# A layer with convolution and sparse attention on one core: the gating product changes engine, the convolution's start is tied to the weight casts, the channel norm is pipelined, and maxima are placed later

## The chip, the cores and the metric

The kernel runs on one core of a Trainium2 chip. The metric is the device time of one execution in microseconds (us). TensorE is called PE below, VectorE DVE, ScalarE ACT, GpSimd POOL, and SyncE, which only issues transfers here, SP. A name such as `gt` in a row is a tile (`gt` those of the gate stage, `cv` the convolution's, `nm` the norm's, `at` the attention's), `scratch_...` is a buffer in DRAM, and a name such as L1042 is a line of the kernel before.

## The reference

One layer over 2048 prompt positions and 64 sample positions, 2112 columns in all, with 1024 channels. What touches the change:

```python
z = h @ w_in
a_conv, g_conv, q, k, v, g_attn, qi, ki, wi, gm = split_in(z)
# conv_branch: u, then a causal depthwise convolution of 31 taps, LayerNorm over channels, silu
u = a[..., :D_CONV] * jax.nn.sigmoid(a[..., D_CONV:])
y = conv(u) + conv_b
y = jax.nn.silu(layernorm(y, ln_g, ln_b))
y_c = (y * jax.nn.silu(g_conv)) @ w_conv_out
# attend_block: for each query the 256 best keys by an index score, then softmax over these
score = jnp.where(admissible[None], score, -jnp.inf)
_, idx = lax.top_k(score, top_k)
```

## The kernel before, in words

The program is a row of stages, each with one instruction stream per engine and a barrier at its end: setup, rows, scores, **gate**, **norm**, **attention**, branch, output. The change lies in the three in bold.

**Gate stage.** PE multiplies the activations `ha` with 56 blocks of 128 weight columns, once for each half of the 2112 columns: blocks 0 to 55 for the first half, 56 to 111 for the second. Block n belongs to pair m = n // 2. One block is 72 matmuls of 352 columns (three split products, L1042), and two PSUM buffers alternate, so PE starts block n only when ACT has evicted block n-2. In the first half POOL splits each block's weights into a high and a low part (`cast`, L600 and L602), and ACT stores both parts to `scratch_ws`; in the second half ACT fetches them back (`fetch`), and issues the fetch for block n+2 right behind the eviction of block n. Each half begins with the eight pairs of kind `u` (pairs 0 to 7 and 28 to 35): one block is the sigmoid part, the other the plain part; ACT evicts them to `stage[0]` and `stage[1]`, and POOL forms their product in `ustage` (`gated`, L1011) and stores it to `scratch_u` (L1014). ACT evicts the next pair only when that product is done. The pair behind the last `u` pair waits in ACT for all `u` products.

Meanwhile ACT and DVE search thresholds for the 256 best keys of each query: 32 rounds of bisection, in each of which ACT counts for the query tiles of the tuple `SCALAR` (L813) and DVE for those of `VECTOR` (L842), after which DVE decides (L850 and following). ACT's rounds stand between its evictions, seven in eight blocks. Then DVE writes the masks (up to L905), and then convolves: eight steps k, four for each half of the columns, each of two channel groups with 31 taps, so 62 instructions (L1168 two, L1172 sixty). The loads of `u` and the stores of `y` are issued by SP; those of step 4 wait for all 16 products to be stored.

**Norm stage.** Five chunks (four of 512 columns, one of 64) of 8 x 128 channels. For each: PE sums (L1232), DVE subtracts the mean (L1269), ACT squares (L1252), PE sums the squares (L1242), DVE adds epsilon (L1275), ACT takes the square root (L1254), DVE the reciprocal (L1278) and one Newton step (L1280 to L1283) and scales (L1284), ACT applies silu (L1257, eight instructions), DVE multiplies with the gate (L1287), POOL stores (L1220). The `y` tiles have two buffers, but each engine's stream goes through one chunk after the other.

**Attention stage.** 68 units (four key-value groups times 17 query tiles) with 308 block pairs, one pair a step. PE's stream is written step by step from a plan: scores of the step's pair (L1602 to L1614), values of the pair two steps earlier (L1633 to L1635), and between them matmuls for the row maxima of a later unit (L1656), which go through a ring of two PSUM banks and are reduced by DVE (L1776). The maxima of unit u need `qhi[u % 3]`, which POOL casts (L1556, L1558) as soon as the last scores of unit u-3 are done. `opens` is the first step in which maxima of unit u may stand: `last[u - 3] + 1`; from there they are dealt two or three to a step, or up to four where they are due. POOL also prepares `near` tiles between the maxima (L1571, L1572), and, inside units 8 to 12 of each group but the last, the keys and values of the next group (L1520 to L1551).

Of the kernel before, what the change touches and what calls it, by code (L numbers as in the profile page):

```python
# [785 lines left out]
class Search:  # L786


    SCALAR = (15, 12, 6, 14, 11, NT)
    VECTOR = (13, 9, 7, 2, 10, 8, 5, 4, 3)  # L790
# [117 lines left out]
def gate_stage(nc, mem, w, scr, scores, kept):  # L908
# [3 lines left out]
    with ExitStack() as ctx:  # L912
# [3 lines left out]
                           + [([P, KC, P], F32R)] * 4 + [([P, W], F32)] * 3  # L916
# [3 lines left out]
        raw, whi, wlo, stage, ustage = parts[1:3], parts[3:5], parts[5:7], parts[7:9], parts[9]  # L920
        junk, equal, junk2, rank = parts[10:14]
        cells = {"count": parts[14], "goal": parts[15], "short": parts[16], "value": parts[17],
                 "candidate": parts[18], "taken": parts[19], "flip": parts[20], "bit": parts[21], "limbs": parts[22]}
        assert mem.at["gt22"] + 20 * ntk <= mem.high([([P, KC, W], F32R)] * 2)
# [80 lines left out]
        def _(pool):  # L1005
            def gated(m):
# [5 lines left out]
                half, _, i = pairs[m]  # L1012
                pool.wait_ge(s_u, u_done[m + 1])
                pool.dma_start(scr["u"][i * P:(i + 1) * P, half * W:(half + 1) * W], ustage[:]).then_inc(s_ustore, 16)  # L1014

            for m, (half, kind, i) in enumerate(pairs):
                for b in range(2):
                    if half == 0:
                        if m:
                            pool.wait_ge(s_wst[b], 32 * m)  # L1020
                        pr.cast(pool, b, m)
                if kind == "u" and i:
                    gated(m - 1)
                if kind == "u" and i == KC - 1:
                    gated(m)

# [35 lines left out]
        def _(act):  # L1062
            def evict(m, b):
# [78 lines left out]
        def _(dve):  # L1142
# [5 lines left out]

            for k in range(8):
# [14 lines left out]
                for k_ in range(CONV_W):  # L1164
                    for e, (c, mine, to) in enumerate(both):
# [7 lines left out]
                        ins.then_inc(s_tap, 1)  # L1173
                dve.wait_ge(s_tap, base + TAPS)
# [3 lines left out]
def norm_stage(nc, mem, out, scr):  # L1178
# [3 lines left out]
    with ExitStack() as ctx:  # L1182
        sem = lambda n: ctx.enter_context(nc.semaphore("norm_" + n))
        CW = 512
        parts = mem.layout("nm", [([P, total + MASKPAD], BF16)] + [([P, KC, CW], F32)] * 5 + [([P, CW], F32)] * 4
                           + [([P, KC, 2, STATE], F32)] + [([STATE, 2, D], F32)])
        y, sq, gc = parts[1:3], parts[3], parts[4:6]
        var, inv, tmp, _ = parts[6:10]
        tails, states = parts[10:12]

        chunks = [(c, c, CW) for c in range(0, SEQ, CW)] + [(SEQ + STATE, SEQ, DEC)]
        s_y, s_gc = [sem("y0"), sem("y1")], [sem("gc0"), sem("gc1")]
        s_store = [sem("store0"), sem("store1")]
        s_mean, s_var, s_sq, s_dve, s_sqrt, s_silu, s_out = (sem(n) for n in ("mean", "var", "sq", "dve", "sqrt", "silu", "out"))
        s_tail, s_tt, s_st = sem("tail"), sem("tt"), sem("st")
        block = ctx.enter_context(nc.Block())
        PER = 8

        @block.sync
        def _(sp):  # L1200
            tail_of = scr["u"].rearrange("(c p) t -> p c t", p=P)
            for k, end in enumerate((SEQ, T)):
                sp.dma_start(tails[:, :, k, :], tail_of[:, :, end - STATE:end]).then_inc(s_tail, 16)
            for n, (col, tok, width) in enumerate(chunks):
                b = n % 2
                if n >= 2:
# [966 lines left out]
```

## Time and profile before

| | us |
|---|---|
| median of 3 runs | 4201.15 |
| lowest and highest | 4200.99 and 4205.64 |
| profiled execution, its own time | 4206.21 |
| its span in the trace | 4204.5 |
| PE busy | 3544.8 (84%) |
| DVE busy | 2776.7 (66%) |
| POOL busy | 1389.7 (33%) |
| ACT busy | 1361.2 (32%) |

The profiled execution took 1.7 us more than its span and 5.1 us more than the median. The busy share of PE is an average over stages; in the gate stage PE is the engine that the others feed, in the norm stage it idles for most of the time.

### The profile page before, as it was taken

To read this page: it belongs to the slowest core of one execution; us is meant where nothing else is said; L and a number is where in the kernel's file an instruction comes from. 1 tells how busy PE (TensorE), PEld (TensorE's weight loads), DVE (VectorE), ACT (ScalarE), POOL (GpSimd) and SP (SyncE) were. 2 spreads that over 40 slices of the span, in tenths; PEclk is the share of its full clock that TensorE was granted. 3 is DMA by queue.
4 is the path that set the end of the run, shared out by engine and by line. 5 is a ranking of instruction groups with operands and counts; after the bars stand their busy time and mean duration, and the time that the engine had idled before them with its cause. 6 is when DMAs were issued, how large, how long until landed. Compare 5 with 4: busy or idle time off the path is not lost. (4 is left out here: it accounts for less than half of the span.)

```text
span 4204.5 us, 49713 instructions
## 1 busy us (share of the span) xinstructions
PE 3544.8 (84%) x18895; PEld 2949.0 (70%) x18895; DVE 2776.7 (66%) x4232; ACT 1361.2 (32%) x1587; POOL 1389.7 (33%) x1050
## 2 busy tenths in 40 slices
PE   5967769899994858999942789989989997899789
PEld 1966559899994858999921455555555554899777
DVE  1412898878999992997034777777877775554244
ACT  2201667667200000010023355545545554000011
POOL 1333324533457271000000464454363342344200
PEclk9988999999997989999976799999999998999999
DMA  7573106545653514444343221201201112465533
GB/s 254 170 268 92 35 18 183 173 158 168 198 184 115 192 50 166 158 155 160 126 147 120 64 51 29 65 26 31 63 26 29 33 31 94 127 227 182 179 109 118
DMA packets 381304, 502.12 MB, mean 119 GB/s; under 512 B 47304, under 2 KB 287064, under 8 KB 380507
## 3 DMA queue, kind: packets, MB, share of 16 engines
q1 hardware_dynamic: 253211, 212.58, 17.1%
q10 hardware_dynamic: 114672, 237.76, 16.9%
q0 software_dynamic: 13264, 49.85, 3.4%
q8 instruction: 78, 1.28, 0.1%
q14 instruction: 79, 0.65, 0.1%
HBM read 306.67 MB, written 199.73 MB: 120 GB/s over the span
## 5 line engine op out<-in xcount | busy, mean ns | idle before, releaser
L1042 PE MATMUL psum<-ha,gt 128*128 128x352 f32 x8064 | 1326.2, 326 | 164.1 <-POOL gt L602 88.4
L1042 PEld LDWEIGHTS psum<-ha,gt 128*128 128x128 f32 x8064 | 1320.2, 190 | 169.9 <-POOL gt L602 78.6
L1172 DVE SCALAR_TENSOR_TENSOR cv<-cv,vecs,cv 128x1056 f32<-128x1056 f32 (+1 forms) x480 | 606.4, 1342 | 0.0
L1827 DVE TENSOR_TENSOR at_plo<-at,at 128x1024 fp32r<-128x1024 f32 (+2 forms) x308 | 390.7, 1269 | 142.5 <-ACT at L1727 141.1
L1726 ACT ACTIVATE at<-psum 128x1024 f32<-128x1024 f32 (+2 forms) x308 | 293.2, 952 | 524.1 <-PE psum L1614 523.9
L1656 PE MATMUL psum<-at,at 128*128 128x512 f32 (+5 forms) x688 | 349.3, 513 | 131.8 <-POOL at L1558 57.1
L613 PE MATMUL psum<-br,br 128*128 128x352 f32 x2304 | 376.1, 325 | 42.4 <-DVE br L1941 41.1
L613 PEld LDWEIGHTS psum<-br,br 128*128 128x128 f32 x2304 | 375.5, 189 | 42.8 <-DVE br L1941 41.2
L842 DVE TENSOR_SCALAR_CACHE_REDUCE gt<-sc,gt 128x1792 bf16<-128x1792 f32 (+9 forms) x294 | 350.1, 1258 | 1.2
L813 ACT ACTIVATE gt<-sc,gt 128x2048 bf16<-128x2048 f32 (+2 forms) x192 | 298.4, 1555 | 67.8 <-issue 59.8
L1079 ACT ACTIVATE gt<-psum 128x1056 f32<-128x1056 f32 x80 | 83.9, 1049 | 716.2 <-PE psum L1042 695.8
L600 POOL TENSOR_TENSOR gt<-gt,ones 128x1024 fp32r<-128x1024 f32 x56 | 183.5, 3277 | 382.3 <-DMA scratch_ws<-gt 180.4
L1727 ACT ACTIVATE at<-psum 128x1024 fp32r<-128x1024 f32 (+2 forms) x308 | 290.8, 944 | 0.0
L1776 DVE CUSTOM_DVE_ANT_0 at<-psum,cv 128x512 bf16<-128x512 f32 (+4 forms) x416 | 237.6, 580 | 75.2 <-PE psum L1656 68.9
L1656 PEld LDWEIGHTS psum<-at,at 128*128 128x128 f32 x688 | 139.2, 203 | 197.1 <-POOL at L1558 71.6
L1602 PE MATMUL psum<-at,at 128*128 128x512 f32 (+1 forms) x580 | 245.5, 423 | 0.0
L1633 PE MATMUL psum<-at,at 128*65 128x512 f32 (+1 forms) x580 | 231.5, 399 | 1.7 <-ACT at L1739 0.8
L1605 PE MATMUL psum<-at,at 66*128 66x512 f32 (+1 forms) x580 | 229.3, 395 | 0.0
L1635 PE MATMUL psum<-at_plo,at 128*65 128x512 f32 (+1 forms) x580 | 227.9, 393 | 0.0
L1634 PE MATMUL psum<-at,at 128*65 128x512 f32 (+1 forms) x580 | 227.5, 392 | 0.0
L1614 PE MATMUL psum<-at,cv 128*128 128x512 bf16 (+1 forms) x580 | 226.4, 390 | 0.0
L1220 POOL DMA_DIRECT2D scratch_c<-nm x5 | 4.5, 897 | 655.0 <-DVE nm L1287 655.0
(229 smaller groups left out, 5236.2 us busy)
## 6 DMA issues: line engine op xcount, KB each, us to landing
scratch_ws<-gt ACTq DMA_DIRECT2D x112, 512.0 KB, 6.1
gt<-scratch_ws ACTq DMA_DIRECT2D x112, 512.0 KB, 5.1
gt<-in_w_in_dram ACTq DMA_DIRECT2D x56, 512.0 KB, 5.3
scratch_gm<-gt ACTq DMA_DIRECT2D x32, 528.0 KB, 3.1
br<-scratch_gm ACTq DMA_DIRECT2D x32, 528.0 KB, 3.6
scratch_m<-br POOLq DMA_DIRECT2D x32, 528.0 KB, 4.4
at<-scratch_q SPq DMA_DIRECT2D x128, 128.0 KB, 2.8
su<-in_ada_w_dram SPq DMA_DIRECT2D x6, 2048.0 KB, 22.3
```

The lines of the kernel that those rows point to most:

```text
L613: last = self.nc.tensor.matmul(self.psum[b][:, j, 0:W // 3], w[b][:, c, :], a[:, c, j * (W // 3):(j + 1) * (W // 3)], start=(c == 0 and k ...
L813: nc.scalar.activation(junks[(done + k) % 2][:, 0:keys_of(t)[1]], part_of(scores, t), ACT.Sign, bias=cells["candidate"][:, j:j + 1].bitcas ...
L842: nc.vector.tensor_scalar(junks[k % 2][:, 0:keys_of(t)[1]], part_of(scores, t), threshold[:, j:j + 1].bitcast(F32), None, compare, ALU.add ...
L1042: ins = nc.tensor.matmul(psum[b][:, j, 0:W // 3], wt[b][:, c, :], a[:, c, j * (W // 3):(j + 1) * (W // 3)], start=(c == 0 and k == 0), sto ...
L1172: ins = nc.vector.scalar_tensor_tensor(to[:, 0:width], mine[:, k_:k_ + width], tap, to[:, 0:width], ALU.mult, ALU.add)
L1602: nc.tensor.matmul(dst, kst[g % 2][:, keys], qhi[u % 3][:, 0:n], start=True, stop=False)
L1633: nc.tensor.matmul(acc[0:VW, 0:n], vst[g % 2][:, v, 0, :], phi[j % 3][:, k, 0:n], start=(b == 0), stop=False)
L1656: nc.tensor.matmul(bank(("max", u, h, c))[:, 0:w], qhi[u % 3][:, at:at + P], kst[g % 2][:, key0:key0 + w], start=True, stop=True).then_inc ...
L1726: nc.scalar.activation(prob[j % 3][:, 0:len(mine), 0:n], src, ACT.Exp)
L1727: nc.scalar.activation(phi[j % 3][:, 0:len(mine), 0:n], src, ACT.Exp).then_inc(s_phi, 1)
L1776: nc.vector.tensor_tensor_reduce(out=junk[r % 2][:, 0:w], in0=bank(("max", u, h, c))[:, 0:w], in1=other, scale=1.0, scalar=LOWEST, op0=ALU ...
L1827: nc.vector.tensor_tensor(plo[j % 3][:, 0:len(mine), 0:n], prob[j % 3][:, 0:len(mine), 0:n], phi[j % 3][:, 0:len(mine), 0:n].bitcast(F32), ...
```

## The change

1. In the search, query tile 6 (896 keys) moves from ACT's tuple to DVE's, so ACT counts five tiles a round and DVE ten.
2. In the second half DVE forms the eight `u` products, each behind a fixed instruction of the convolution (behind number 96 + 18j, counted from 0 over all steps k); POOL only stores them. ACT evicts the `u` pairs of the second half alternately to `stage[0..1]` and `stage[2..3]`, so it may be one pair further ahead of the products. The pair behind the last `u` pair still waits for all of them.
3. DVE starts the convolution only when POOL has split the last weight block (number 55).
4. The norm has four `y` buffers, two PSUM banks for means and two for squares; the chunks are interleaved on each engine; the square root and reciprocal become exp(-0.5 ln(x)) on ACT, with the Newton step kept on DVE.
5. In the attention's plan the maxima of a unit open up to two steps later.

```diff
-    SCALAR = (15, 12, 6, 14, 11, NT)
-    VECTOR = (13, 9, 7, 2, 10, 8, 5, 4, 3)
+    SCALAR = (15, 12, 14, 11, NT)
+    VECTOR = (13, 9, 7, 2, 6, 10, 8, 5, 4, 3)
...
+            for m in range(half_pairs, half_pairs + KC):
+                store(m)
...
                 if kind == "u":
-                    if u_done[m] and b == 0:
+                    at = stage[b + 2 * (half * (m % 2))]
+                    if half == 0 and u_done[m] and b == 0:
                         act.wait_ge(s_u, u_done[m])
-                    if o_done[m]:
+                    if half and i >= 2 and b == 0:
+                        act.wait_ge(s_u, u_done[m] - 1)
+                    if half and o_done[m]:
                         act.wait_ge(s_store[b], 16 * o_done[m])
-                    nc.scalar.activation(thirds(stage[b], W // 3), psum[b][:, :, 0:W // 3], ACT.Copy if b else func).then_inc(pr.s_read, 1)
+                    nc.scalar.activation(thirds(at, W // 3), psum[b][:, :, 0:W // 3], ACT.Copy if b else func).then_inc(pr.s_read, 1)
                     return
                 if b == 0 and pairs[m - 1][1] == "u":
                     act.wait_ge(s_u, u_done[m])
...
+            def gated(m):
+
+                e = 2 * (m % 2)
+                dve.wait_ge(pr.s_read, 2 * (m + 1))
+                dve.wait_ge(s_ustore, 16 * u_done[m])
+                nc.vector.tensor_tensor(ustage[:], stage[e][:], stage[e + 1][:], ALU.mult).then_inc(s_u, 1)
+
+            dve.wait_ge(pr.s_split, BLOCKS)
+            gated_at = {96 + 18 * j: half_pairs + j for j in range(KC)}
...
+                        if step in gated_at:
+                            gated(gated_at[step])
+                        step += 1
...
+            load_y(0)
+            load_y(1)
+            load_gc(0)
...
+            load_y(2)
+            load_gc(1)
+            load_y(3)
...
+            for n in range(2, N):
+                load_gc(n)
+                if n + 2 >= YB and n + 2 < N:
+                    load_y(n + 2)
...
+            sums(0)
+            sums(1)
+            for n in range(N):
+                squares(n)
+                if n + 2 < N:
+                    sums(n + 2)
...
+                nc.scalar.activation(r, var[n % 2][:, 0:width], ACT.Ln, bias=eps[:]).then_inc(s_root, 1)
+                act.wait_ge(s_root, 2 * n + 1)
+                nc.scalar.activation(r, r, ACT.Exp, scale=-0.5).then_inc(s_root, 1)
...
+            square(0)
+            for n in range(N):
+                if n + 1 < N:
+                    square(n + 1)
+                root(n)
+                if n:
+                    swish(n - 1)
+            swish(N - 1)
...
+            centre(0)
+            centre(1)
+            for n in range(N):
+                scale(n)
...
+                if n + 2 < N:
+                    centre(n + 2)
+                if n:
+                    gated(n - 1)
+            gated(N - 1)
...
-            opens = self.last[u - 3] + 1 if u >= 3 else self.begin
+            opens = max(self.last[u - 3] + 1, min(self.last[u - 3] + 3, self.first[u] - 7)) if u >= 3 else self.begin
```

On DVE, in the convolution's step k = 1 of the changed kernel, the first of the eight products (L1162; `gt_4589` and `gt_4590` are `stage[0]` and `stage[1]`) stands here:

```order
L1190 SCALAR_TENSOR_TENSOR cv_4615<-cv_4611,vecs,cv_4615 128x1056
L1190 SCALAR_TENSOR_TENSOR cv_4614<-cv_4610,vecs,cv_4614 128x1056
L1162 TENSOR_TENSOR gt_4593<-gt_4589,gt_4590 128x1056
L1190 SCALAR_TENSOR_TENSOR cv_4615<-cv_4611,vecs,cv_4615 128x1056
L1190 SCALAR_TENSOR_TENSOR cv_4614<-cv_4610,vecs,cv_4614 128x1056
L1190 SCALAR_TENSOR_TENSOR cv_4615<-cv_4611,vecs,cv_4615 128x1056
```

It has 97 instructions of the convolution ahead of it; the eighth has 223. In the kernel before this product was POOL's, behind nothing.

On ACT in the norm stage, one chunk before (`nm_9344` is the squares' tile, `nm_9347` and `nm_9348` hold the variance and its root):

```order
L1252 ACTIVATE nm_9344<-nm_9342 128x4096
L1254 ACT_TABLE_LOAD
L1254 ACTIVATE nm_9348<-nm_9347 128x512
L1257 ACT_TABLE_LOAD
L1257 ACTIVATE nm_9342<-nm_9342,vecs 128x512 x8
```

and in the changed kernel, from the squares of the third chunk to the silu of the first:

```order
L1303 ACTIVATE nm_9347<-nm_9343 128x4096
L1311 ACT_TABLE_LOAD
L1311 ACTIVATE nm_9349<-psum,nm_9354 128x512
L1313 ACT_TABLE_LOAD
L1313 ACTIVATE nm_9349<-nm_9349 128x512
L1319 ACT_TABLE_LOAD
L1319 ACTIVATE nm_9341<-nm_9341,vecs 128x512 x8
```

The silu now works on a chunk two behind that of the squares, and there are three table loads for two.

On PE in the attention, at step 1 (scores of unit 1, then the shift row of unit 2 that both have; maxima of unit 3, whose `opens` was step 1), before:

```order
L1614 MATMUL psum<-at_9748,cv_4605 128x512
L1656 MATMUL psum<-at_9706,at_9721 128x512
L1602 MATMUL psum<-at_9722,at_9706 128x512
L1605 MATMUL psum<-at_9725,at_9708 128x512
L1614 MATMUL psum<-at_9748,cv_4605 128x512
L1656 MATMUL psum<-at_9706,at_9721 128x512
L1666 MATMUL psum<-at_9749,at_9746 66x128 x4
```

and the same scores in the changed kernel:

```order
L1705 MATMUL psum<-at_9753,cv_4607 128x512
L1693 MATMUL psum<-at_9727,at_9711 128x512
L1696 MATMUL psum<-at_9730,at_9713 128x512
L1705 MATMUL psum<-at_9753,cv_4607 128x512
L1757 MATMUL psum<-at_9754,at_9751 66x128 x4
```

The two maxima are gone from here and stand two steps later. Over the plan, 60 of the 68 units open two or three steps later; steps with four maxima go from 16 to 50, and steps with none from 27 to 60.

## Rows read from the trace of the kernel before

**Rows 1.** Busy time by stage; columns: PE, PEld, DVE, ACT, POOL, PEclk, DMA share, GB/s

```profile
1284.00:1592.00 308.00, 174.79 (x1011) 171.17 (x1012) 297.51 (x238) 16.58 (x16) 179.95 (x15) 0.79 0.30 110
...
2107.00:2307.00 200.00, 74.32 (x176) 35.15 (x176) 85.13 (x50) 57.62 (x62) 4.73 (x6) 0.68 0.38 135
...
2345.00:3545.00 1200.00, 1105.33 (x5087) 684.61 (x5087) 916.71 (x2131) 622.76 (x750) 533.27 (x671) 0.97 0.15 37
```

**Rows 2.** Timeline of PE, gate stage: start, duration, [idle before <- releaser]

```profile
1179.78 103.92 PE L1042 MATMUL psum<-ha,gt 128*128 128x352 f32 x641
1344.56 25.44 PE L1042 MATMUL psum<-ha,gt 128*128 128x352 f32 x144 [60.86 <-POOL gt L602]
...
1394.76 35.18 PE L1042 MATMUL psum<-ha,gt 128*128 128x352 f32 x216 [2.01 <-DMA gt<-scratch_ws]
1434.91 49.56 PE L1042 MATMUL psum<-ha,gt 128*128 128x352 f32 x288 [4.97 <-DMA gt<-scratch_ws]
1511.87 48.70 PE L1042 MATMUL psum<-ha,gt 128*128 128x352 f32 x288 [27.40 <-DMA gt<-scratch_ws]
1591.24 8.99 PE L1042 MATMUL psum<-ha,gt 128*128 128x352 f32 x45 [30.66 <-DMA gt<-scratch_ws]
```

**Rows 3.** Timeline of POOL, the same stretch

```profile
1273.40 68.34 POOL L600 TENSOR_TENSOR gt<-gt,ones 128x1024 fp32r<-128x1024 f32 x1 [8.47 <-DMA scratch_ws<-gt]
...
1462.34 42.17 POOL L1011 TENSOR_TENSOR gt<-gt,gt 128x1056 f32<-128x1056 f32 x1 [24.25 <-ACT gt L1073]
```

**Rows 4.** Timeline of DVE: end of the masks, a convolution step of each half

```profile
1258.62 0.20 DVE L1146 MEMSET cv<- 128x30 f32 x4
...
1266.16 73.83 DVE L1172 SCALAR_TENSOR_TENSOR cv<-cv,vecs,cv 128x1056 f32<-128x1056 f32 x60
...
1890.13 75.72 DVE L1172 SCALAR_TENSOR_TENSOR cv<-cv,vecs,cv 128x1086 f32<-128x1086 f32 x60
```

**Rows 5.** Timeline of ACT: an eviction that waited for POOL's product

```profile
1504.59 1.05 ACT L1073 ACTIVATE gt<-psum 128x1056 f32<-128x1056 f32 x1 [42.34 <-POOL gt L1011]
```

**Rows 6.** Waits from 620 to 1100 us: total, times, longest

```profile
DVE gt L850 <- ACT gt L813: 79.6, 26, 17.1
...
PE psum L1042 <- POOL gt L602: 27.5, 4, 11.8
```

**Rows 7.** Timeline of DVE: a count over 896 keys

```profile
1086.62 1.14 DVE L842 TENSOR_SCALAR_CACHE_REDUCE gt<-sc,gt 128x896 bf16<-128x896 f32 x1
```

**Rows 8.** Timelines of PE, DVE and ACT in the norm stage

```profile
2122.43 9.37 PE L1232 MATMUL psum<-nm,mean_ones 128*128 128x512 f32 x16 [15.57 <-DMA nm<-scratch_y]
...
2179.39 9.91 PE L1242 MATMUL psum<-nm,mean_ones 128*128 128x512 f32 x16 [23.41 <-ACT nm L1252]
...
2131.84 4.42 DVE L1269 TENSOR_TENSOR nm<-nm,psum 128x4096 f32<-128x4096 f32 x1 [165.99 <-PE psum L1232]
...
2153.99 0.69 DVE L1280 TENSOR_TENSOR nm<-nm 128x512 f32<-128x512 f32 x1
...
2175.72 3.62 ACT L1252 ACTIVATE nm<-nm 128x4096 f32<-128x4096 f32 x1 [8.88 <-DVE nm L1269]
...
2190.78 1.28 ACT L1257 ACT_TABLE_LOAD   x1
2201.34 5.74 ACT L1257 ACTIVATE nm<-nm,vecs 128x512 f32<-128x512 f32 x8 [9.29 <-DVE nm L1284]
```

**Rows 9.** DMA issues in the norm stage: KB each, us from issue to landing

```profile
scratch_c<-nm POOLq DMA_DIRECT2D x4, 2048.0 KB, 7.5
```

**Rows 10.** Attention: waits; first and last of six long ones; POOL preparing keys

```profile
PE psum L1656 <- POOL at L1558: 49.8, 28, 6.1
...
2473.42 0.50 PE L1656 MATMUL psum<-at,at 128*128 128x512 f32 x1 [3.29 <-POOL at L1558]
...
3118.44 0.79 PE L1656 MATMUL psum<-at,at 128*128 128x512 f32 x1 [5.63 <-POOL at L1558]
...
2506.30 3.90 POOL L1536 TENSOR_TENSOR at<-at,at_ktmp 64x1600 fp32r<-64x1600 f32 x1
```

More of the change, by code:

```diff
@@ L1005, in _, with store @@
         def _(pool):
+            def store(m):
+                half, _, i = pairs[m]
+                pool.wait_ge(s_u, u_done[m + 1])
+                pool.dma_start(scr["u"][i * P:(i + 1) * P, half * W:(half + 1) * W], ustage[:]).then_inc(s_ustore, 16)
             def gated(m):
@@ L1011, in gated @@
                 nc.gpsimd.tensor_tensor(ustage[:], stage[0][:], stage[1][:], ALU.mult).then_inc(s_u, 1)
[L1012 to L1016, printed above, removed]
+                store(m)
+            for m in range(half_pairs):
                 for b in range(2):
[L1018 to L1022, printed above, removed]
+                    if m:
+                        pool.wait_ge(s_wst[b], 32 * m)
+                    pr.cast(pool, b, m)
+                if pairs[m][1] == "u" and m:
                     gated(m - 1)
-                if kind == "u" and i == KC - 1:
+                if m == KC - 1:
                     gated(m)
+            for m in range(half_pairs, half_pairs + KC):
+                store(m)
         @block.tensor
@@ L1192, in norm_stage @@
-        s_y, s_gc = [sem("y0"), sem("y1")], [sem("gc0"), sem("gc1")]
-        s_store = [sem("store0"), sem("store1")]
-        s_mean, s_var, s_sq, s_dve, s_sqrt, s_silu, s_out = (sem(n) for n in ("mean", "var", "sq", "dve", "sqrt", "silu", "out"))
+        sem = mem.signals(ctx, "norm_")
+        CW, YB, GB = 512, 4, 2
+        parts = mem.layout("nm", [([P, total + MASKPAD], BF16)] + [([P, KC, CW], F32)] * (YB + GB + 1) + [([P, CW], F32)] * 4
+                           + [([P, KC, 2, STATE], F32), ([STATE, 2, D], F32), ([P, 1], F32)])
@@ new lines, in norm_stage @@
+        y, gc, sq = parts[1:1 + YB], parts[1 + YB:1 + YB + GB], parts[1 + YB + GB]
+        inv, tmp = parts[2 + YB + GB:4 + YB + GB], parts[4 + YB + GB:6 + YB + GB]
+        tails, states, eps = parts[6 + YB + GB:]
+        chunks = [(c, c, CW) for c in range(0, SEQ, CW)] + [(SEQ + STATE, SEQ, DEC)]
+        N = len(chunks)
+        s_y, s_store = [sem(f"y{i}") for i in range(YB)], [sem(f"store{i}") for i in range(YB)]
+        s_gc = [sem(f"gc{i}") for i in range(GB)]
+        s_eps, s_mean, s_diff, s_sq, s_var, s_root, s_step, s_unit, s_silu, s_out = (
+            sem(n) for n in ("eps", "mean", "diff", "sq", "var", "root", "step", "unit", "silu", "out"))
@@ L1239, in _, with square @@
                         last.then_inc(s_tt, 1)
-                pe.wait_ge(s_sq, n + 1)
-                for c in range(KC):
-                    last = nc.tensor.matmul(mem.bank(1)[:, 0:width], mem.mean_ones[:], sq[:, c, 0:width], start=(c == 0), stop=(c == KC - 1))
-                last.then_inc(s_var, 1)
         @block.scalar
         def _(act):
-            for n, (col, tok, width) in enumerate(chunks):
-                b = n % 2
-                act.wait_ge(s_dve, PER * n + 1)
+            def square(n):
+                width = chunks[n][2]
+                act.wait_ge(s_diff, n + 1)
```

128 lines of the change are left out of this document (74 added, 54 removed).

## The prediction

> **What bounds the kernel now.** I read the busy time by stage first. From 1284 to 1592 us PE is busy for 175 of 308 us and its granted clock averages 0.79; in the norm stage (2107 to 2307) PE is busy for 74 of 200 us and DVE for 85, so nothing is full; in the attention PE is busy for 1105 of 1200 us at 0.97 [rows 1]. These are the three places that the change touches, and they have different limits.
>
> The timeline of PE shows what the first gap is made of. Up to 1283.7 PE runs 641 matmuls in 103.92 us, 11.67 us for a block of 72. Then it idles for 60.9 us until POOL has split block 54, and later for 5.0, 27.4 and 30.7 us for fetched weights [rows 2]. The timeline of POOL names the cause of all four: a split that lies under the convolution takes 68.34 us, and a product 42.17 us [rows 3]. In the same time DVE runs 60 convolution instructions in 73.83 us without a gap [rows 4]. POOL gets through when DVE pauses between two steps k. ACT waits for the product (42.34 us) and issues the next fetch only behind its eviction: eviction at 1504.59, PE at 1511.87, so 7.3 us later [rows 2, 5]. Each long stall also makes the next blocks slower: the two blocks at 1344.56 take 25.4 us where 23.3 are due, the four at 1511.87 take 48.7 instead of 46.7 [rows 2], about 2 us each.
>
> **Gate stage, what goes.** No split and no product on POOL lies beside the convolution any more. That removes 60.9 + 5.0 + 27.4 + 30.7 = 124.0 us and three slow restarts, 6: together 130 us.
>
> **Gate stage, what comes instead.** The start of the convolution, on the clock of before: block 53 ends at 1283.7, the split of block 55 needs that end and some 4.5 us, so DVE starts at about 1288.3. The masks are ready at 1258.6 [rows 4], so this wait costs DVE 24 us (it had started at 1264), which nobody waits for so far. One convolution instruction is 73.83/60 = 1.23 us, two first ones together 2.1 and the clears 0.2, so a step k takes 76.1 us; number 96 ends 119 us behind the start, at 1407.3. The product is a two-input operation over 1056 columns; by 4.42 us for 4096 [rows 8] it takes 1.2 us and is ready at 1408.5.
>
> PE meanwhile: without the stall block 54 starts at 1283.7. Before, 1344.56 to 1394.76 passed from block 54 to block 57, 50.2 us, of which 2 were the slow restart; so block 57 starts at 1331.9, and 58 to 61 end at 1390.2 (five blocks from there). The eviction of block 60, first of pair 30, needs product 28. PE can't start block 62 before 1408.5 + 7.3 = 1415.8: a new stall of 25.6 us. From then on products come every 18 x 1.23 + 1.2 = 23.4 us and PE wants one pair every 23.3 us. The product that a pair needs arrives about 2.5 us behind the end of its first block, and with 7.3 us for the fetch that is inside the 11.67 us of the second block: no further stall, but no recovery either.
>
> Behind the last `u` pair, pair 36 still waits for all products. Its first block would end at about 1546, and the eighth product is behind number 222: 3 x 76.1 + 45.4 + 8 x 1.2 us behind the start, at 1572. Block 73 ends at 1557.6, block 74 starts at 1579.3: a second new stall of 22 us. With 2 us each for the restarts the new stalls are 51 us. Net of this: 130 - 51 = **79 us**.
>
> DVE ends its half 0 at 1288.3 + 4 x 76.1 + 8 x 1.2 = 1602, the loads of step 4 start some 10 us behind the eighth product (1582) and are in by then, and four steps of 75.72 + 1.9 [rows 4] end at 1913. PE ends the stage at 2107 - 79 = 2028, so the convolution stays hidden with 115 us to spare.
>
> **The search.** DVE waits for ACT's counts for 79.6 us in 26 of 32 rounds [rows 6]. Tile 6 costs DVE 1.14 us a round [rows 7], 37 us in all, which lie in that wait; ACT loses about as much per round and keeps up with PE better. PE's waits for POOL in this time are 27.5 us, 11.8 of them the start of the stage [rows 6], which stays. The others come from late evictions and late stores in part. I take 4 us of gain, bounds 0 and 10.
>
> **Norm stage.** Durations [rows 8]: sums 9.4 us at the lower clock, squares' sums 7 to 9.9, a wide DVE operation 4.42, a narrow one 0.69, squares 3.62, table load 1.28, silu 5.74. The two operations that replace root and reciprocal do not exist before; ln and exp of 512 columns are bounded by nothing below and by silu's 5.74/8 = 0.72 us for as many columns above, and I take 0.63 us. Each has a table load in the order. From the first load of SP as zero: first `y` 9, sums to 18, centre to 22.5; second sums to 26, centre to 30.6; first sums of squares to 34, second squares to 37.7, root with two loads to 41; scale (four narrow and one wide) to 48.7, copies to 51, third centre to 55.5. Then the loop repeats: squares 3.6, load, ln, load, exp 3.8, scale 7.1, centre 4.4 give 19 us a chunk on a cycle DVE, ACT, DVE; the product of the chunk before (4.4) fills the time that DVE waits for ACT's squares and root. So the fourth centre ends at 74.6, the first product at 79, the third scale at 89.2. The last chunk's `y` needs the first store, 1.2 + 7.5 us [rows 9], and 3 for itself: 91; its sums stand in PE's stream ahead of the fourth chunk's squares, which PE finishes at about 101 instead of 86. Root to 106, scale to 113, products to 117.5 and, behind the silu at 123.4, 127.8; the store lands at 136.5. The stage had 195 us from its first transfer to the next stage, and has about 138: **57 us** less. Bounds: 45, if the transfers crowd (each 2 MB store took 7.5 us by itself), and 75, if that last chunk does not hold PE.
>
> A rule weighed against this: a table load takes 1.28 us in the timeline [rows 8]. The Trainium skill (ScalarE: Activation LUTs, What ACT_TABLE_LOAD costs) puts a switch at about 2.66 us with its drain; by that the five ln-exp pairs would cost some 7 us more and the forecast would be 7 us later. The same page (Table sets) says that one set holds both ln and exp, so that one load would serve both; the order shows two, and with one the forecast would be 6 us earlier.
>
> **Attention.** PE waits 49.8 us for POOL's query casts, 28 times. Six of these are long (3.3, 4.6, 4.3, 6.1, 4.3 and 5.6 us, 28.2 together) and lie where POOL prepares the next group's values and keys between the near tiles of units 8 and 10 and the casts of units 9 and 11 (one such operation takes 3.9 us, three to four stand in a row) [rows 10]. There POOL is late by its own work, which begins when the maxima of the unit before are reduced; these move by the same two steps, and between them and the first maximum of the next unit there are 2.25 steps before and 2 after. So these 28 us stay. The other 22 waits, 21.6 us, are casts that start with the buffer's release, and two steps (7 us and more) hide 1.9 us of cast. Against it stands the bunching: DVE is busy for 917/308 = 3.0 us in a mean step and PE for 3.6 us [rows 1], with 2.2 maxima; 1.8 more of them, at 0.69 us each for a narrow operation [rows 8], bring DVE to 4.2 us, and at 0.5 us each [rows 10], partly overlapped, PE to about the same. 34 more such steps at 0.2 us are 7. I take **14 us**, bounds -15 (each bunched step 1 us late) and +45 (the long waits go too).
>
> **Sum.** 79 + 4 + 57 + 14 = 154 us. Against the profiled execution's own 4206.2 that is 4052; it stood 5 us above the median of 4201.15, so I forecast 4201 - 154 = **4047 us**. A difference of 0.2% is 8 us here, about what a measurement of this kernel can tell from none.
>
> **Rivals.**
> - *The products do not hold PE* (some other order of events lets ACT run ahead, or DVE's start is earlier). For it: both stalls hang on a few us per product. Against: the waits stand in the code, and 97 and 223 instructions at 1.23 us are fixed. The saving would be 205 us: 3996. Chance 0.10.
> - *The bunched maxima turn against the gain*: DVE becomes late in the attention, 15 us lost instead of 14 won: 4076. For it: three times as many steps with four. Against: DVE is busy for 917 of 1200 us [rows 1]. Chance 0.12.
> - *The norm's interleaving is held by transfers or by the last chunk*, saving only 30 us: 4074. Chance 0.12.
> - *The convolution becomes the stage's bound, and the kernel is slower.* It must end 154 us plus 115 us later than worked out: over 496 instructions 0.54 us more each, 1.77 us instead of 1.23. Rows of it show 1.23 and 1.26 us, even beside POOL [rows 4], so this asks for a contention that none shows. 4210 or more. Chance 0.02.
> - *The change does not do what it says*: the last splits are still held up, now under the mask operations, and a stall of 60 us stays: 4107. Splits before 1264 show no such length. Chance 0.03.
> - The forecast within its own range of 4025 to 4068: 0.61.
>
> The range of 4005 to 4082 takes in the two middle rivals and part of the first. Faster by over 0.2%: 0.97; within 0.2%: 0.01; slower: 0.02.
>
> **What would show it.** No POOL split above 6 us; the convolution's first instruction a few us behind the last split; PE gaps of about 25 us before block 62 and 22 us before block 74, each ended by a fetch; the second-half products on DVE 1.2 us each, 23.4 apart; the norm stage about 138 us long, with PE idle before the fourth chunk's squares; in the attention the six long waits for L1558's successor still there and the short ones gone. The forecast is wrong if the fetch behind a held eviction takes much more than 7 us, if the second new stall is missing, or if steps with four maxima last over 5 us.

## The result, and the profile after

The changed kernel takes 4064.68 us (median of 4 runs, 4064.11 to 4065.72), the kernel before on the same chip 4203.4 us (4200.99 to 4205.98). The ratio is 0.9658 with a 95% interval of 0.9631 to 0.9684, so 138.7 us less by the medians. The forecast was 154 us less and a range of 4005 to 4082 us.

Stage by stage, from the first row of one stage to the first row of the next in the two traces (the gate stage from its first matmul):

| stretch | before, us | after, us | less | forecast |
|---|---|---|---|---|
| gate stage, search included | 1483.3 | 1398.8 | 84.5 | 79 + 4 |
| norm stage | 195.1 | 143.7 | 51.4 | 57 |
| attention, first to last score | 1189.5 | 1186.6 | 2.9 | 14 |
| all else | 1336.6 | 1334.9 | 1.7 | 0 |
| span | 4204.5 | 4064.0 | 140.5 | 154 |

The same stages in the changed kernel, as busy times of a stretch; the columns are those of [rows 1].

```profile
629.50:2028.30 1398.80, 1322.46 (x8064) 1318.42 (x8064) 1199.77 (x1400) 381.89 (x429) 286.69 (x134) 0.97 0.50 165
2028.30:2172.00 143.70, 66.58 (x176) 32.11 (x176) 67.74 (x37) 64.61 (x70) 4.62 (x7) 0.74 0.53 184
2218.50:3405.10 1186.60, 1089.08 (x5060) 678.77 (x5058) 892.67 (x2104) 619.81 (x748) 533.95 (x665) 0.98 0.15 37
```

**Gate stage.** The timeline of PE in the changed kernel (L1047 is the matmul, L1042 before), at block 57, block 62 and block 74:

```profile
1330.11 60.07 PE L1047 MATMUL psum<-ha,gt 128*128 128x352 f32 x360 [2.04 <-DMA gt<-scratch_ws]
1413.46 142.77 PE L1047 MATMUL psum<-ha,gt 128*128 128x352 f32 x864 [23.28 <-DMA gt<-scratch_ws]
1577.91 72.26 PE L1047 MATMUL psum<-ha,gt 128*128 128x352 f32 x430 [21.68 <-DMA gt<-scratch_ws]
```

The four stalls of [rows 2] are gone and two new ones stand in their place, 23.3 and 21.7 us, at 1413.5 and 1577.9 us (forecast: 25.6 and 22, at 1415.8 and 1579.3). The timelines of POOL, DVE and ACT, in this order, say why:

```profile
1282.68 1.89 POOL L600 TENSOR_TENSOR gt<-gt,ones 128x1024 fp32r<-128x1024 f32 x1 [6.49 <-PE psum L1047]
```
```profile
1287.11 0.12 DVE L1177 MEMSET cv<- 128x30 f32 x2 [29.46 <-POOL gt L602]
...
1404.88 1.25 DVE L1162 TENSOR_TENSOR gt<-gt,gt 128x1056 f32<-128x1056 f32 x1
...
1566.65 1.25 DVE L1162 TENSOR_TENSOR gt<-gt,gt 128x1056 f32<-128x1056 f32 x1
```
```profile
1406.21 1.05 ACT L1081 ACTIVATE gt<-psum 128x1056 f32<-128x1056 f32 x1 [38.25 <-DVE gt L1162]
...
1567.98 1.05 ACT L1087 ACTIVATE gt<-psum 128x1056 f32<-128x1056 f32 x1 [33.98 <-DVE gt L1162]
```

The last two blocks' splits (first parts) take 1.9 us each, where that of block 54 took 68.34 [rows 3], and DVE starts the convolution 0.1 us behind the last of them. The first product stands behind 97 instructions of the convolution and comes at 1404.9; ACT evicts at 1406.2, and PE gets its weights at 1413.5, 7.3 us later. The eighth product and the second stall are the same chain again, but longer: ACT evicts at 1568.0 and PE goes on at 1577.9, 9.9 us later. Here the evicted block is no `u` block, so ACT issues its store (at 1569.1) ahead of the fetch (at 1569.5).

**Norm stage.** Timelines of ACT (third chunk), PE, SP and POOL in the changed kernel:

```profile
2082.61 3.62 ACT L1303 ACTIVATE nm<-nm 128x4096 f32<-128x4096 f32 x1 [13.71 <-DVE nm L1342]
2086.25 1.28 ACT L1311 ACT_TABLE_LOAD   x1
2087.54 0.69 ACT L1311 ACTIVATE nm<-psum,nm 128x512 f32<-128x512 f32 x1
2088.25 1.28 ACT L1313 ACT_TABLE_LOAD   x1
2089.54 0.63 ACT L1313 ACTIVATE nm<-nm 128x512 f32<-128x512 f32 x1
...
2101.64 3.62 ACT L1303 ACTIVATE nm<-nm 128x4096 f32<-128x4096 f32 x1 [4.39 <-DVE nm L1342]
```
```profile
2122.82 3.67 PE L1271 MATMUL psum<-nm,mean_ones 128*128 128x64 f32 x16 [29.40 <-DMA nm<-scratch_y]
2126.28 8.64 PE L1280 MATMUL psum<-nm,mean_ones 128*128 128x512 f32 x16
```
```profile
2105.97 0.39 SPq L1234 DMA_DIRECT2D nm<-scratch_gc  x1
2119.69 0.39 SPq L1228 DMA_DIRECT2D nm<-scratch_y  x1
```
```profile
2106.24 0.92 POOL L1259 DMA_DIRECT2D scratch_c<-nm  x1 [77.84 <-DVE nm L1364]
```

A chunk now takes 19.0 us (squares at 2082.61 and 2101.64), as worked out. The last chunk holds PE, as forecast, but longer: the first store (the row of POOL) is issued at 2106.24, and SP can issue the load behind it only at 2119.69, 13.4 us later.

**Attention.** Waits of PE from 2210 to 3410 us in the changed kernel: us in total, times, longest (L1649 is the query cast, L1558 in [rows 10]; L1894 and L1906 are the row and column operations of DVE that share the ring of banks, L1867 the reduction of the maxima):

```profile
PE psum L1747 <- POOL at L1649: 43.7, 16, 6.3
PE psum L1747 <- DVE at L1894: 20.4, 33, 1.8
PE psum L1747 <- DVE at L1906: 13.1, 21, 2.0
PE psum L1747 <- DVE at L1867: 10.1, 25, 0.9
```

Of the 28 waits of [rows 10], 22 short ones (21.6 us) have become 8 (8.5 us). The six long ones (28.2 us) have become eight of 2.7 to 6.3 us (35.2 us). The waits for DVE's row and column operations went from 11.0 and 15.7 to 20.4 and 13.1 us, so PE's waits for the cast, the rows and the columns are no shorter in total (76.5 us before, 77.2 after). What is 7.6 us shorter is PE's busy time in this stretch, 1089.1 us where it was 1096.7, for the same 5060 matmuls; why, no run shows. The longest of all, on the timelines of POOL and of PE:

```profile
2380.82 4.41 POOL L1627 TENSOR_TENSOR at<-at,at_ktmp 64x1600 fp32r<-64x1600 f32 x1
2385.29 0.61 POOL L1647 CAST at<-at 128x512 fp32r<-128x512 f32 x1
2385.98 1.25 POOL L1649 TENSOR_TENSOR at<-at,at 64x512 fp32r<-64x512 f32 x1
```
```profile
2387.29 0.80 PE L1747 MATMUL psum<-at,at 128*128 128x512 f32 x1 [6.27 <-POOL at L1649]
```

The cast starts 0.06 us behind the preparation of the keys and ends at 2387.2, where PE has stood since 2381.0.

### The profile page after: what moved, and what is told of

Same layout as the page of the kernel before. It is cut to its first block and busy times, and to the rows that moved or that the text cites. A ratio compares the mean times of both kernels' runs of the same rounds, so it can differ in the third digit from the quotient of the medians.

```text
span 4064.0 us, 49727 instructions
## 1 busy us (share of the span) xinstructions
PE 3526.9 (87%) x18895; PEld 2946.4 (72%) x18895; DVE 2772.5 (68%) x4292; ACT 1334.8 (33%) x1532; POOL 1208.8 (30%) x1043
## 3 DMA queue, kind: packets, MB, share of 16 engines
q8 instruction: 78, 1.28, 0.1%
## 5 line engine op out<-in xcount | busy, mean ns | idle before, releaser
L1047 PE MATMUL psum<-ha,gt 128*128 128x352 f32 x8064 | 1322.5, 326 | 83.3 <-DMA gt<-scratch_ws 47.0
L1047 PEld LDWEIGHTS psum<-ha,gt 128*128 128x128 f32 x8064 | 1318.4, 190 | 87.2 <-issue 58.0
L1747 PE MATMUL psum<-at,at 128*128 128x512 f32 (+5 forms) x688 | 339.2, 499 | 154.2 <-DVE at L1848 51.4
L842 DVE TENSOR_SCALAR_CACHE_REDUCE gt<-sc,gt 128x1792 bf16<-128x1792 f32 (+5 forms) x325 | 383.2, 1246 | 1.2
L813 ACT ACTIVATE gt<-sc,gt 128x2048 bf16<-128x2048 f32 (+9 forms) x160 | 265.5, 1660 | 80.7 <-DVE gt L858 56.7
L1867 DVE CUSTOM_DVE_ANT_0 at<-psum,cv 128x512 bf16<-128x512 f32 (+4 forms) x416 | 236.7, 580 | 74.8 <-PE psum L1747 67.2
L1662 POOL CAST at<-cv 128x256 f32<-128x256 bf16 (+1 forms) x240 | 119.7, 499 | 506.4 <-DVE at L1867 505.5
L1724 PE MATMUL psum<-at,at 128*65 128x512 f32 (+1 forms) x580 | 240.0, 414 | 2.9 <-ACT at L1830 1.1
L600 POOL TENSOR_TENSOR gt<-gt,ones 128x1024 fp32r<-128x1024 f32 x56 | 118.1, 2109 | 386.9 <-PE psum L1047 236.6
L1725 PE MATMUL psum<-at,at 128*65 128x512 f32 (+1 forms) x580 | 229.1, 395 | 0.0
```

The lines of the kernel that those rows point to most:

```text
L813: nc.scalar.activation(junks[(done + k) % 2][:, 0:keys_of(t)[1]], part_of(scores, t), ACT.Sign, bias=cells["candidate"][:, j:j + 1].bitcas ...
L842: nc.vector.tensor_scalar(junks[k % 2][:, 0:keys_of(t)[1]], part_of(scores, t), threshold[:, j:j + 1].bitcast(F32), None, compare, ALU.add ...
L1047: ins = nc.tensor.matmul(psum[b][:, j, 0:W // 3], wt[b][:, c, :], a[:, c, j * (W // 3):(j + 1) * (W // 3)], start=(c == 0 and k == 0), sto ...
L1724: nc.tensor.matmul(acc[0:VW, 0:n], vst[g % 2][:, v, 0, :], phi[j % 3][:, k, 0:n], start=(b == 0), stop=False)
L1747: nc.tensor.matmul(bank(("max", u, h, c))[:, 0:w], qhi[u % 3][:, at:at + P], kst[g % 2][:, key0:key0 + w], start=True, stop=True).then_inc ...
L1867: nc.vector.tensor_tensor_reduce(out=junk[r % 2][:, 0:w], in0=bank(("max", u, h, c))[:, 0:w], in1=other, scale=1.0, scalar=LOWEST, op0=ALU ...
```

## Experiments

Each is measured against the kernel before on its own chip, where that took 4209 to 4218 us in the median. Differences of a few us between medians are therefore read together with the stage in the trace.

| edit of the changed kernel (the sixth: of the kernel before) | us | ratio to before | interval |
|---|---|---|---|
| pair behind the last u pair relaxed | 4042.03 | 0.9588 | 0.9558 to 0.9618 |
| products at 50 + 18j | 4017.21 | 0.9528 | 0.9498 to 0.9557 |
| no wait for the last split | 4079.55 | 0.9678 | 0.9641 to 0.9715 |
| search tuples of before | 4068.53 | 0.9651 | 0.9626 to 0.9677 |
| norm stage of before | 4112.38 | 0.9760 | 0.9724 to 0.9795 |
| before, with the wait for the last split | 4220.34 | 1.0007 | 0.9980 to 1.0033 |
| fifth y buffer | 4046.12 | 0.9602 | 0.9567 to 0.9636 |
| opens of before | 4069.64 | 0.9653 | 0.9627 to 0.9680 |
| maxima one step later | 4055.83 | 0.9630 | 0.9591 to 0.9669 |
| preparation behind the query cast | 4041.03 | 0.9587 | 0.9552 to 0.9621 |
| the same, opens of before | 4067.04 | 0.9656 | 0.9616 to 0.9696 |
| products earlier, fifth buffer, preparation behind | 3972.92 | 0.9435 | 0.9405 to 0.9465 |

### The two new stalls of the gate stage

```diff
                 if b == 0 and pairs[m - 1][1] == "u":
-                    act.wait_ge(s_u, u_done[m])
+                    act.wait_ge(s_u, u_done[m] - half)
```

> The changed kernel with the pair behind the last u pair waiting for all products but one (its stage tiles are free then). Theory: the stall of 21.7 us before block 74 and its slow restart of 2 us go: 4041 us. The stall of 23.3 us before block 62 stays. Rival: something else behind the same pair holds the next fetch (the eighth product, a store), and the stall only moves: 4060 us or more.

Measured 4042.03 us, and in its trace the gate stage takes 1373.3 us instead of 1398.8. PE waits 23.0 us before block 62 and never more than 1 us behind it until 1700 us: the second stall hangs on that one wait.

```diff
-            gated_at = {96 + 18 * j: half_pairs + j for j in range(KC)}
+            gated_at = {50 + 18 * j: half_pairs + j for j in range(KC)}
```

> The changed kernel with the eight products of DVE at convolution instructions 50 + 18j instead of 96 + 18j, so 57 us earlier. Theory: each product comes a few us behind its pair's eviction, both new stalls (23.3 and 21.7 us) and their slow restarts (2 us each) go: about 4016 us, 4012 to 4022. Rival: DVE is now the one that waits for evictions, and POOL's stores or the fetches keep PE waiting some 10 us: 4030 us. Rival 2: only the first stall goes: 4040 us.

Measured 4017.21 us; the gate stage takes 1349.4 us. PE's timeline of this run, from block 57 to 1515 us:

```profile
1331.18 184.03 PE L1047 MATMUL psum<-ha,gt 128*128 128x352 f32 x1126 [2.08 <-DMA gt<-scratch_ws]
```

Both stalls are gone: PE runs 1126 matmuls from 1331.2 to 1515.2, where the window ends, without a gap, and none above 1 us follows up to 1700. DVE's first product is at 1350.0 here. The place of the product in DVE's stream set both stalls.

### What the wait for the last split is worth, and what it is worth alone

```diff
-            dve.wait_ge(pr.s_split, BLOCKS)
             gated_at = {96 + 18 * j: half_pairs + j for j in range(KC)}
```

> The changed kernel without DVE's wait for the last weight split: the convolution starts at about 1264 us again, beside the splits of blocks 54 and 55. Theory: the split of block 54 takes some 68 us again and PE stalls 61 us before block 54, but the products then are due 38 us earlier against PE, so that the stalls before blocks 62 and 74 (45 us with 4 us of restarts) go: 12 to 17 us more than the changed kernel, 4077 to 4082 us. Rival: the stalls add up: 4127 us. Second rival: the splits were slow for another reason (the products behind them), and without those they are short: 4040 us or less.

Measured 4079.55 us; the gate stage takes 1408.6 us. POOL, PE and DVE in this run:

```profile
1272.27 68.58 POOL L600 TENSOR_TENSOR gt<-gt,ones 128x1024 fp32r<-128x1024 f32 x1 [8.23 <-DMA scratch_ws<-gt]
```
```profile
1343.67 25.44 PE L1047 MATMUL psum<-ha,gt 128*128 128x352 f32 x144 [60.87 <-POOL gt L602]
```
```profile
1406.65 1.26 DVE L1162 TENSOR_TENSOR gt<-gt,gt 128x1056 f32<-128x1056 f32 x1 [18.13 <-ACT gt L1081]
```

The stall is back, 60.87 us against 60.86, now without any product on POOL. DVE reaches the first product before its pair is evicted, so it waits 18.1 us for ACT and PE waits for no product at all. So this stall and the other two do not add up. The wait for the split wins the difference, 15 us by the medians and 9.8 us of the gate stage in the traces. What it wins where the products come early was not run.

```diff
+            dve.wait_ge(pr.s_split, BLOCKS)
             for k in range(8):
                 half = k // 4
```

> The kernel before with one edit: DVE starts the convolution only when POOL has split the last weight block; the products stay on POOL in both halves. Theory: the stall of 61 us goes, but POOL's eight products of the second half now all lie under the convolution, 42 us or more each where PE wants a pair every 23.3 us; PE waits some 15 to 20 us a pair for most of them, so 100 us or more come in place of 61 + 63: the kernel is no more than 30 us faster than before, 4170 to 4230 us. Rival: the wait alone gives most of the gate stage's gain, and the products' move little: 4140 us or less.

Measured 4220.34 us, no difference from before that is clear of the noise; in the trace the gate stage takes 1499.0 us instead of 1483.3. POOL's products and PE's stalls in this run:

```profile
1374.61 67.45 POOL L1011 TENSOR_TENSOR gt<-gt,gt 128x1056 f32<-128x1056 f32 x1 [9.08 <-DMA scratch_u<-gt]
...
1452.20 67.26 POOL L1011 TENSOR_TENSOR gt<-gt,gt 128x1056 f32<-128x1056 f32 x1 [9.26 <-DMA scratch_u<-gt]
...
1526.42 2.87 POOL L1011 TENSOR_TENSOR gt<-gt,gt 128x1056 f32<-128x1056 f32 x1 [6.09 <-DMA scratch_u<-gt]
```
```profile
1374.76 25.88 PE L1042 MATMUL psum<-ha,gt 128*128 128x352 f32 x144 [9.52 <-DMA gt<-scratch_ws]
1451.96 24.94 PE L1042 MATMUL psum<-ha,gt 128*128 128x352 f32 x144 [51.32 <-DMA gt<-scratch_ws]
1526.59 48.45 PE L1042 MATMUL psum<-ha,gt 128*128 128x352 f32 x288 [49.69 <-DMA gt<-scratch_ws]
1606.41 72.66 PE L1042 MATMUL psum<-ha,gt 128*128 128x352 f32 x432 [31.37 <-DMA gt<-scratch_ws]
```

The stall before block 54 is gone, and 9.5 + 51.3 + 49.7 + 31.4 = 141.9 us have come behind it, where [rows 2] had 5.0 + 27.4 + 30.7 = 63.1. The two edits are not worth the same. DVE's products without the wait already bring the gate stage from 1483.3 to 1408.6 us, 74.7 of the 84.5 us; the wait adds the rest, and only behind them. Alone it moves the convolution onto POOL's products and the stage is 15.7 us longer in the trace.

### The search

> The changed kernel with query tile 6 counted by ACT again, as before. Theory (the forecast's term of 4 us): 4069 us, 4065 to 4075. Rival: ACT's counts never hold PE, no difference: 4063 to 4066 us. Second rival: the masks are ready earlier by 1 us with the old split, and since the convolution waits for the last weight split anyway nothing follows from it.

The edit puts the two tuples of before back. Measured 4068.53 us. From the stage's first matmul to block 57 PE takes 702.7 us here and 701.2 in the run of the kernel before with the split wait, which has the old tuples too. It takes 700.6 in the changed kernel and 699.6 to 701.8 in the nine other runs with its tuples and the split wait. The term of 4 us is about 2 us, at most 3, and neither these runs nor the medians tell it surely from none.

### The norm stage

> The changed kernel with the norm stage of before (two y buffers, square root and reciprocal, one chunk after the other). Theory from the traces: the norm stage went from 195 to 143.7 us, 51.4 less: 4116 us. Rival, the forecast's term: 57 us, 4122 us. Second rival: part of the 51 us is a transfer that the shorter gate stage brought nearer, and the old norm costs less than that here: 4100 us.

The edit is the old norm stage, whole. Measured 4112.38 us. The stage takes 195.2 us here (from 2027.55 to 2222.75), as before, so the shorter gate stage in front of it changes nothing, and the term is 51.4 us. The edit takes buffers, interleaving and the new root back together; what each is worth was not run.

```diff
-        CW, YB, GB = 512, 4, 2
+        CW, YB, GB = 512, 5, 2
...
             load_gc(1)
             load_y(3)
+            load_y(4)
```

> The changed kernel with a fifth y buffer of 64 columns for the last chunk of the norm, loaded right behind the fourth, so that its load waits for no store. Theory: PE's idle 29.4 us before the last chunk's sums, which stand ahead of the fourth chunk's squares, goes; these squares end some 20 us earlier and the stage is 18 us shorter: 4047 us, 4043 to 4051. Rival: the end of the stage is set by the transfers of the gates and the stores, and at most 5 us are won: 4060 us.

Measured 4046.12 us. PE of this run:

```profile
2092.02 1.89 PE L1272 MATMUL psum<-nm,mean_ones 128*128 128x64 f32 x16
2104.07 8.87 PE L1281 MATMUL psum<-nm,mean_ones 128*128 128x512 f32 x16 [10.15 <-ACT nm L1304]
```

The last chunk's sums run at 2092.0 instead of 2122.8, and the fourth chunk's squares follow at 2104.1. The stage ends 18.0 us earlier (125.7 us long). What held it was one 64-column load behind a store.

### The attention

> The changed kernel with one edit undone: the maxima of a unit open right behind the release of its query buffer, as before. The changed kernel took 4064.7 us. Theory from the trace of the changed kernel: the later maxima won 2.9 us in the attention, because the long waits for POOL (28.2 us before) grew to 35 us and waits for DVE grew by 9 us while the short waits for POOL went (21.6 to 8.5 us); so about 4068 us, 4062 to 4073. Rival, the forecast's term of 14 us: 4079 us. Second rival, the later maxima are a loss beside this norm and gate stage: under 4060 us.

The edit puts the `opens` of before back. Measured 4069.64 us, 5 us more by the medians; the attention takes 1189.5 us in its trace, as before, against 1186.6. The term is 2.9 us.

```diff
-            opens = max(self.last[u - 3] + 1, min(self.last[u - 3] + 3, self.first[u] - 7)) if u >= 3 else self.begin
+            opens = max(self.last[u - 3] + 1, min(self.last[u - 3] + 2, self.first[u] - 7)) if u >= 3 else self.begin
```

> The changed kernel with the maxima opening one step later than before instead of two (57 units move by one step; 28 steps have four maxima, where the changed kernel has 50 and the one before 16). Theory: one step of 3.7 us covers a cast of 1.9 us, so the short waits for POOL stay away, the long ones stay as they are, and half of the bunching's price is saved: 4059 us. Rival: the bunching costs nothing, and less room for POOL makes the long waits no shorter: 4065 us or more.

Measured 4055.83 us, attention 1177.6 us. Its waits:

```profile
PE psum L1747 <- POOL at L1649: 39.3, 18, 5.4
PE psum L1747 <- DVE at L1894: 27.0, 29, 2.5
PE psum L1747 <- DVE at L1906: 5.3, 14, 1.0
PE psum L1747 <- DVE at L1867: 3.5, 11, 0.4
```

With 28 steps of four maxima instead of 50, one step of delay is worth 12 us (1189.5 - 1177.6), and the second costs 9 of them. The waits for DVE on these three lines are 35.8 us instead of 43.6, those for POOL 39.3 instead of 43.7. By single waits, those above 2.5 us for the cast are 28.2 us in total before, 22.9 here and 35.2 in the changed kernel. So the second step brings back long waits for POOL as well as waits for DVE; how much of its price is the bunching was not taken apart.

```diff
                 if u:
                     queries(u)
+                    w = u - 1
+                    if w % NTL in parts_of_group and w // NTL + 1 < KV:
+                        parts_of_group[w % NTL](w // NTL + 1)
                     nears(u)
-                if u % NTL in parts_of_group and u // NTL + 1 < KV:
-                    parts_of_group[u % NTL](u // NTL + 1)
```

> The changed kernel with one edit in POOL's attention stream: the preparation of the next group's values, keys and bias stands behind the query cast of the next unit instead of ahead of it. Theory: with the later maxima this cast has 7 us of slack, so the long waits for it (eight, 35 us) go, and the tiles behind it, needed a step later, are mostly hidden too: 25 to 32 us less, 4036 us. Rival: the near tiles behind the preparation are then late by the same 7 us and hold DVE's reductions and so PE's ring: 4060 us or more.

Measured 4041.03 us, attention 1162.5 us. Its waits:

```profile
PE psum L1748 <- DVE at L1895: 37.4, 38, 4.0
...
PE psum L1748 <- POOL at L1649: 4.8, 4, 1.9
```

The waits for the cast fall from 43.7 to 4.8 us, all eight long ones included. Part of it comes back as waits for DVE's row operations, which are 17 us more, two of them 4.0 us long. The rival's reason is not theirs: DVE's reductions wait for `near` tiles for 1.2 us in all. Timelines of POOL and DVE ahead of the first of the two, at 2386.3:

```profile
2380.96 3.57 POOL L1627 TENSOR_TENSOR at<-at,at_ktmp 64x1600 fp32r<-64x1600 f32 x1
```
```profile
2381.03 3.52 DVE L1882 TENSOR_TENSOR at<-at,at 128x4 fp32r<-128x4 f32 x1
```

A DVE operation on four columns lasts as long as the POOL operation that began 0.07 us ahead of it, and the row operation stands behind it in DVE's stream. That is the one wait; the other 37 were not followed.

> POOL's preparation behind the next query cast as in the run at 4041.0 us, but with the maxima opening right behind the release, as before. Theory: the later maxima are what gives the cast and the tiles behind the preparation their slack, and they are worth their 14 us (the short waits of 21.6 us less the bunching) once the preparation is out of the cast's way, where they were worth 3 us beside it: 4055 us, 4050 to 4062. Rival: they are worth 3 us here too: 4044 us.

The same edit on top of the `opens` of before. Measured 4067.04 us, attention 1187.5 us. Neither number expected came out. Its waits:

```profile
PE psum L1748 <- DVE at L1907: 34.1, 38, 3.9
PE psum L1748 <- DVE at L1868: 26.6, 30, 4.4
PE psum L1748 <- POOL at L1649: 15.2, 16, 1.9
```

The waits of DVE itself name what is late instead:

```profile
DVE at L1868 <- POOL at L1663: 32.0, 25, 5.8
```

Without the room of two steps the moved preparation only changes which tile is late. PE's waits for the cast go from 49.2 (in the run with the `opens` of before) to 15.2 us, DVE's for the `near` tiles (L1663) from 6.9 to 32.0, and PE's for these lines of DVE from 26.8 to 60.7. So the rival of the run with the `opens` of the change, a `near` tile that is late in the cast's place, is what happens here. The two edits are worth 3 and 2 us alone and 27 together (1189.5 to 1162.5).

### All three at once

> The changed kernel with the three edits that won one by one: DVE's products at 50 + 18j, the fifth y buffer, POOL's preparation behind the next query cast. They lie in three stages one after the other, so the theory is that they add up: 4064.7 - 47.5 - 18.6 - 23.7 = 3975 us, 3970 to 3982. Rival: less, since a stage that starts with other transfers in flight gives part of it back: 3990 us.

Measured 3972.92 us, 0.9435 of before. The three edits add up, and this version beats both kernels. In its gate stage PE's granted clock is 0.99, against 0.97 in the changed kernel and 0.95 before:

```profile
629.50:1975.00 1345.50, 1314.98 (x8064) 1311.51 (x8062) 1199.07 (x1398) 381.50 (x429) 285.99 (x134) 0.99 0.51 171
```

## Why the prediction was right, and where its terms were off

The direction, the range and the order of the terms held; the sum was 13.5 us too large by the traces, 15 by the medians.

**Gate stage, right (79 forecast; 84.5 measured, of which the search has up to 3).** The chain was found in its parts before: splits and products that are slow only under the convolution, 7.3 us from eviction to matmul, 97 and 223 instructions of 1.23 us ahead of the products. Both stalls came within 2.4 us of their size and their place, and the experiments removed the second by its wait and both by earlier products. That the second stall was met so closely is in part luck: the eighth product came 4.1 us earlier than worked out (1567.9, not 1572), and PE goes on 2.7 us later behind it (10.0 us, not 7.3, with the store ahead of the fetch). The rival that the products don't hold PE fell with them. The rival that the last splits are still held fell with splits of 1.9 us. So did the rival of the convolution as the bound: it ends at 1908.9, 114 us ahead of PE. One reading was too narrow: "POOL gets through when DVE pauses between two steps k" holds for most of its operations but not for all, as the last section shows; no term hung on it.

**Search, small (4 forecast, up to 3 measured, none not ruled out).** Two PE gaps near 1050 us, 2.2 and 1.1 us, come back with the old tuples.

**Norm stage, 57 forecast, 51.4 measured.** The loop of 19 us a chunk is exact. The step that was mis-sized is "The last chunk's `y` needs the first store, 1.2 + 7.5 us, and 3 for itself": the load took 3.1 us, but the store and what lies around it 13.4, which is 4.7 of the 5.6 us. SP issued a 2 MB gate load at 2105.97, 0.3 us ahead of that store, and the stage's 2 MB stores land in 10.7 us in the median, where they took 7.5 before. That loads and stores crowd each other is likely, and no run takes it apart. The stage saved 51 us, so the rival of 30 us fell; the last chunk did hold PE, as the sum already had it.

Of the two rules weighed there neither moved the time. The first instruction behind a table load starts 0.01 us after the load's 1.28 us, and root with two loads took 3.9 us where 3.8 was worked out from rows. The Trainium skill (ScalarE: Activation LUTs, What ACT_TABLE_LOAD costs) would have had 7 us more with one drain for each of the five pairs, and 14 with one behind each of their two loads; the trace shows neither. By the same page (Table sets) one load could serve ln and exp; the trace shows one for each, so the 6 us less did not come either.

**Attention, 14 forecast, 2.9 measured: the term that was mis-sized most.** The step reads "So these 28 us stay". The short waits shrank to 8.5 us, 13.1 won. The long ones did not stay, they grew to 35.2 us, 7.0 lost: eight waits instead of six. The longest of each group hardly moved (4.6, 6.1 and 5.6 us before, 6.3, 6.0 and 4.9 after). The waits for DVE's rows and columns grew from 26.7 to 33.5 us. Together these losses use up the 13.1 us; the 2.9 us that are left show in PE's busy time. The bunching's price of 7 can't be told apart: the second step of delay costs 9 in the run above, long waits for POOL included. The rival that the bunched maxima lose 15 us did not come, but the term is nearer to nothing than to its forecast. The long waits were put down to the right cause: moved behind the cast, the preparation costs none of them. What was missed, as far as the order of POOL's stream says, is that they hang on the pace of the maxima too: POOL begins to prepare when those of one unit are reduced and must be done when those of the next begin, and they were dealt closer together. This is argued, not shown. The run with one step (28 steps of four maxima, long waits of 22.9 us) fits it, but there they are shorter than with none (28.2 us), so pace is not all.

What stays open: why DVE's row operations hold PE for longer when maxima open later (L1894, 11.0 to 20.4 us, and 27.0 with one step). No run separates their place in the ring from the number of maxima.

## What to carry to other kernels

When work moves into another engine's stream, count the instructions ahead of it and compare with when its consumer wants it: here 46 places in DVE's stream were worth 47 us by the medians and 49 in the gate stage's trace. Slack given to a consumer is worth only what its producer doesn't spend at once; two edits that gave 3 and 2 us alone gave 27 together, so an edit that seems to do little should be read with the next wait in the chain before it is dropped. And a small piece of work behind a buffer's release, like the last 64 columns of the norm, deserves a buffer of its own: 2 KB a partition gave 18 us.

## What the runs showed of the hardware

A POOL operation that meets the convolution does not run slowly, it waits, most often for DVE's pause between two steps. In the run of the kernel before with the split wait, DVE does this around 1440 us:

```profile
1365.96 73.82 DVE L1173 SCALAR_TENSOR_TENSOR cv<-cv,vecs,cv 128x1056 f32<-128x1056 f32 x60
1439.86 0.12 DVE L1160 MEMSET cv<- 128x30 f32 x2
1440.02 3.43 DVE L1169 TENSOR_SCALAR cv<-cv,vecs 128x1056 f32<-128x1056 f32 x2
```

Its 60 instructions take 73.8 us while POOL waits (73.82 here) and with no POOL operation at all (73.85 in the changed kernel). The product that POOL began at 1374.6 ends at 1442.1, 2.3 us behind the last of them; without the convolution beside it such a product takes 2.4 to 2.5 us. The other way round it holds too: DVE's next two instructions take 3.43 us together where the first step's took 1.57, and in the attention a DVE operation on four columns took 3.52 us beside one of POOL.

It is not a rule without exceptions. The product at 1526.4 us in the same run begins 5.6 us after DVE has begun its sixty, and takes 2.87 us. One DVE instruction beside it takes 3.50 us instead of 1.23, and the sixty take 76.03. In the two kernels whose products are POOL's in the second half, twelve POOL operations begin inside the sixty; four get in between two instructions like that one (the other three at 1346.9, 1434.7 and 1511.7 us in the kernel before), and eight wait 17 to 68 us. What decides it the rows do not show.

The Trainium skill (SBUF — State Buffer, SBUF: two separate sides) says that the two engines share a port pair that one of them holds for a whole instruction, for DVE when it has two SBUF inputs. The trace agrees for single instructions (3.50 us of DVE beside 2.87 of POOL). It adds that many such instructions in a row can keep a waiting POOL operation out for as long as they last, 67.4 us here.
